# Three device-memory copies moved from the head of the attention to behind the first up projection's loads

## The reference

```
ext = jnp.concatenate([buf, new_g], axis=1)     # buf: (8 sequences, rows, 2, 4, 64)
new_bufs.append(ext[:, T:])                      # T = 8 new rows, rows = 128, 256, 256
```

## Time and profile before

| | |
|---|---|
| median of 3 runs | 1692.43 us (1685.87 to 1697.28) |
| profiled execution | 1691.04 us, span 1689.3 us |
| TensorE matmul busy | 1584.1 us (94%) |
| VectorE busy | 927.2 us (55%) |
| ScalarE busy | 558.7 us (33%) |
| mean granted TensorE clock | 0.97 of full |
| DMA moved | 155.80 MB, mean 92 GB/s |

### The profile page before, as it was taken

How to read it: one execution, slowest core, us unless ns; L and a number is a source line. 1 busy time by engine, 2 the same in 40 slices (tenths; PEclk the granted TensorE clock), 3 DMA queues, 4 the chain that set the end, 5 groups by cost and what they waited for, 6 DMA issues and landing times.

```text
span 1689.3 us, 24438 instructions
## 1 busy us (share of the span) xinstructions
PE 1584.1 (94%) x9462; PEld 1376.8 (82%) x9462; DVE 927.2 (55%) x1764; ACT 558.7 (33%) x1040; POOL 57.3 (3%) x89
## 2 busy tenths in 40 slices
PE   6999899888899999999979999989989999999995
PEld 5888766656799999987869888856879999998784
DVE  3644243015766666653562286566576666665355
ACT  2222244331333333333222433342133333333321
POOL 0002200000100000000010000000010000000000
PEclk9999899988999999999989899999989999999998
DMA  4223650435222232232221221054122223224211
GB/s 165 97 94 107 233 216 4 137 109 129 70 81 74 77 97 75 74 120 77 78 83 52 66 80 55 26 176 121 50 70 80 74 77 97 75 74 122 75 63 56
DMA packets 150848, 155.80 MB, mean 92 GB/s; under 512 B 7598, under 2 KB 120366, under 8 KB 150542
## 3 DMA queue, kind: packets, MB, share of 16 engines
q1 hardware_dynamic: 146842, 141.70, 27.1%
q0 software_dynamic: 3936, 13.14, 2.4%
HBM read 142.99 MB, written 21.91 MB: 98 GB/s over the span
## 4 chain that ended last, share of the span: by engine, by line
PE 85%; DVE 8%; ACT 4%; issue 2%; DMA 0%; SPq 0%; POOL 0%; DVEq 0%; ACTq 0%; POOLq 0%
PE ps L618 65%; PE ps L599 5%; PE ps L629 4%; PE ps L680 2%; PE ps L787 2%; PE ps L950 1%; DVE x_reg L1570 1%; PE ps L983 1%; PE ps L1014 1%; DVE w_lo L1379 1%; ACT w_hi L1062 1%; DVE x_reg L1574 1%; ACT arena L1095 1%; PE ps L714 1%; DVE arena L1464 1%
## 5 line engine op out<-in xcount | busy, mean ns | idle before, releaser
L618 PE MATMUL ps<-xh_reg,w_hi 128*128 128x288 f32 x1552 | 463.4, 299 | 8.2 <-DVE xl_reg L1386 8.2
L618 PE MATMUL ps<-xl_reg,w_hi 128*128 128x288 f32 x1552 | 458.8, 296 | 0.0
L618 PE MATMUL ps<-xh_reg,w_lo 128*128 128x288 f32 x1552 | 458.8, 296 | 0.0
L618 PE MATMUL ps<-w_hi,xh_reg 128*128 128x512 f32 x768 | 308.7, 402 | 7.9 <-DVE x_reg L1552 3.6
L618 PE MATMUL ps<-w_lo,xh_reg 128*128 128x512 f32 x768 | 302.7, 394 | 0.0
L618 PE MATMUL ps<-w_hi,xl_reg 128*128 128x512 f32 x768 | 302.4, 394 | 0.0
L618 PEld LDWEIGHTS ps<-xh_reg,w_hi 128*128 128x128 f32 x1552 | 293.2, 189 | 10.5 <-DVE xl_reg L1386 5.4
L618 PEld LDWEIGHTS ps<-xl_reg,w_hi 128*128 128x128 f32 x1552 | 293.3, 189 | 0.0
L618 PEld LDWEIGHTS ps<-xh_reg,w_lo 128*128 128x128 f32 x1552 | 292.9, 189 | 0.0
L1379 DVE TENSOR_TENSOR w_lo<-raw,w_hi 128x2048 fp32r<-128x2048 f32 (+1 forms) x52 | 113.7, 2186 | 260.3 <-ACT w_hi L1062 260.3
L618 PEld LDWEIGHTS ps<-w_hi,xh_reg 128*128 128x128 f32 x768 | 146.5, 191 | 40.8 <-issue 8.7
(11 more groups left out here) (176 smaller groups left out, 1649.8 us busy)
## 6 DMA issues: line engine op xcount, KB each, us to landing
raw<-in_ffn_w_up SPq DMA_DIRECT2D x88, 512.0 KB, 5.0
raw<-in_ffn_w_down SPq DMA_DIRECT2D x40, 512.0 KB, 4.6
raw<-in_attn_w_in SPq DMA_DIRECT2D x24, 512.0 KB, 5.0
raw<-in_gla_w_in SPq DMA_DIRECT2D x24, 512.0 KB, 4.4
out_swa_s<-in_state_swa_kv SPq DMA_DIRECT2D x2, 3968.0 KB
x_reg<-in_x_prompt SPq DMA_DIRECT2D x8, 512.0 KB, 5.1
raw<-in_gla_w_out SPq DMA_DIRECT2D x8, 512.0 KB, 4.6
arena<-in_state_swa_kv SPq DMA_DIRECT2D x12, 256.0 KB, 3.3
```

What stands on the lines that cost most here:

```text
L618: mm = pe.matmul(out, lhs(i, a), rhs(i, b), start=first and i == 0 and a + b == 0, stop=last and i == ks - 1 and a == 1)
```

## The change

The loop that issues the three copies is taken from behind the value loads of sequences 0 to 3 and put between `ffn_up(0)` and `ffn_down(0, 2)`. Nothing else differs.

```
@@ head of the attention, SyncE @@
             for s in range(4):
                 cache_rows(s, 1)
 
-            for g in range(3):
-                rows = io[f"state_swa{g}_kv"].shape[2]
-                sp.dma_start(io[f"swa{g}_s"][0, :, 0:rows - T_NEW].rearrange("s r a h d -> s (r a h d)"),
-                             io[f"state_swa{g}_kv"][0, :, T_NEW:rows].rearrange("s r a h d -> s (r a h d)")).then_inc(kv_stored, 16)
             for s in range(2, SEQS):
                 cache_rows(s, 0)
@@ first ConvFFN, SyncE @@
             load_ln(0, "mix", 0)
             ffn_up(0)
+
+            for g in range(3):
+                rows = io[f"state_swa{g}_kv"].shape[2]
+                sp.dma_start(io[f"swa{g}_s"][0, :, 0:rows - T_NEW].rearrange("s r a h d -> s (r a h d)"),
+                             io[f"state_swa{g}_kv"][0, :, T_NEW:rows].rearrange("s r a h d -> s (r a h d)")).then_inc(kv_stored, 16)
             ffn_down(0, 2)
```

## The result

The changed kernel takes 1708.57 us (median of 4 runs, 1707.14 to 1711.06) against 1690.54 us for the kernel before on the same chip (4 runs, 1685.87 to 1697.28): ratio 1.0105, 95% interval 1.0066 to 1.0144, so 11 to 24 us slower. The profiled execution took 1707.14 us, its span is 1705.3 us.

What follows compares the result with a forecast made beforehand. TensorE was taken as the bound (85% of the span, 65% the projections' three products). Old place 0, stall 16.3 and clock 5.0 gave 21.3 us on 1691.04, so 1712.3; medians run 1.4 higher: 1713.7 us, range 1700 to 1724.

Steps and rivals of the forecast that it cites:

- Nothing back at the old place: In the attention, where the copies ran before: removing them gains 0, with 2.7 us as the bound for a gain.
- Rival D: Faster: contention in the attention was real and the new place is free; 2.7 us gained, 1690 us; chance 0.02.
- Copies of 46.9 us from the end of up21's load, in order of issue: Between up and down projection: copies run about 685 to 731.9; the first down load waits behind them, landing at 735.6.
- Rival A: Not slower: engines take turns between a copy and the load behind it, which lands by about 702; 1692 us; chance 0.11.
- Who waits: Start of the down projection: ScalarE waits for the first down load, then VectorE; TensorE starts 7.75 us after landing.
- Stall 16.3: TensorE starts the down projection at 743.35 against 727.05, a stall of 16.3 us.
- One stall: Later down loads: the second lies 3.7 us behind the first, TensorE has 13 us per unit, so no second stall.
- Rival C: Slower by more: the second down unit's low part comes too late, adding some 8 us, 1722 us; chance 0.05.
- Rival B: Not slower: copies use all sixteen engines at 351 GB/s, 28.7 us, first down load lands at 717.4; 1692 us; chance 0.03.
- the cover: Last up unit's matmuls hide the first down load and following work; it may land up to 719.3 for nothing.
- The clock, 5.0 us: After TensorE's gap before the down projection: 9.9 us at half rate, 5.0 us lost, bounds 0 and 6.5.

Runs made afterwards that it cites:

- two copies: Changed kernel, but with the 1920 KB copy left in the old place and only the two of 3968 KB moved: 1701.14 us, ratio 1.0089.
- sixteen engines: Changed kernel with all three copies moved, but each row cut in sixteen and that dimension put first: 1691.01 us, ratio 1.0017.
- the first kernel with GpSimd's queue: Changed kernel, but the three copies issued by GpSimd in its own queue at the same moment, in long runs: 1702.37 us, ratio 1.0079.
- its twin with rows: Copies issued by GpSimd at the same moment, but written as rows of 2 KB instead of long runs: 1703.32 us, ratio 1.0076.

## Why the prediction was right

The forecast was 1713.7 us, 21.3 more than before; measured are 18.0 and 22.6 us in two sets.

- **Nothing back at the old place**: right, by the kernel without copies (ratio 1.0018) and 36.52 us busy in the traces with the copies and without. Rival D falls.
- **Copies of 46.9 us from the end of up21's load, in order of issue**: right. The landing was put at 735.6 in a frame in which up21 ends at 725.16; here everything stands 4.1 us earlier, and 731.5 compares with the measured 731.90. Rival A, that engines take turns between a copy and a load behind it, falls on one queue; with two queues turns there are, and with long packets they do not help. That order of issue holds rests on the landing, on the slope, and on the packets from 708 to 726 in the changed kernel, while down0 and down1 are both outstanding:
```profile
DMA packets 71, 4.00 MB, mean 222 GB/s; under 512 B 8, under 2 KB 8, under 8 KB 8
```
63 long ones of the copies, and not one of the loads' pieces of 2 KB.
- **Who waits**: TensorE 7.75 us after the landing; measured 7.66 in both traces of the changed kernel, 7.65 with two copies, 7.67 with sixteen engines. Stall 16.3, measured 16.6 and 16.9.
- **One stall**: right; down1 follows in 754.22 to 765.11 without a gap. Rival C falls.
- **Rival B**: the mechanism is real, but not in this kernel. With sixteen engines the copies do fit under the cover but for 0.4 us; the arithmetic from 351 GB/s had down0 down at 717.4, measured are 720.06. The price from the Trainium skill that the prediction sets beside it (page "DMA: Bandwidth & Descriptors", section on the anatomy of one DMA) is there a fit for transfers that GpSimd issues; these were issued by SyncE.
- **The clock, 5.0 us**: the one term that was mis-sized. It fell, in the gap, but was back some 3 us after work went on, not 9.9: 1.5 us in one execution, 2.9 in another, 1.4 to 3.0 behind the other stalls. I had read its price off one gap, and one gap says little about the moment of the return. Stall and clock of the two traces add up to 18.1 and 19.8 us, so the 21.3 was 1.5 to 3.2 too high; that it lies between the two measured differences is luck.

## What to carry to other kernels

A bulk transfer that nothing waits for is charged to the first load that must get past it: compare its whole length (bytes over the measured rate) with the time between that load's issue and its first user, and mind that the first user may be an engine that stands in order ahead of other work. Look at the DMA share of the copy alone: here 0.50 went with a first dimension of 8, and 1.03 with one of 16. Another queue helped only when the bulk transfer's packets were short as well (4 KB beside a load in pieces of 2 KB; 63 KB did not do); check the packets' sizes, as rows that touch were joined.

## What was not expected of the hardware

- A queue of its own did not protect a load: 38.7 us to land beside 63 KB packets, and, for down0, 35.5 us beside such packets but 13.6 us beside 4 KB packets, with the engines full in both (alone: 4.5).
- GpSimd's queue put the three copies on more engines at once than SyncE's: its own packets had a share of 99.4% and moved 7.51 MB from 684 to 706, 341 GB/s, for copies whose first dimension is 8, where SyncE's queue showed 0.50 and 215 GB/s. Which copy went to which engines was not looked into.
- SyncE itself was held up when its loads could not move: in the first kernel with GpSimd's queue one issue of a down load took 10.6 us, and 13.1 in its twin with rows, where others take 0.4.
- The same stage took some 3.5 us more in one execution than in another, by the moment at which 2.4 GHz came back around 375 to 385.
